# Projecting the second memory's keys and values beside the norms of the even and the odd layer

## The reference, cut to what matters

```python
mem_n = rmsnorm(mem, g_mem)                       # once, for both layers
# in the even and in the odd layer:
mk, mv = jnp.split(mem_n @ w_mem_kv, 2, axis=-1)  # 256 x 1024 @ 1024 x 1024
sc = einsum('bshd,bmhd->bhsm', q, mk) * HEAD_DIM ** -0.5
out = einsum('bhsm,bmhd->bshd', softmax(sc), mv)
```

## Time and profile before

| | |
|---|---|
| timed runs, us | 3944.46, 3948.77, 3956.41 |
| profiled execution, us | 3957.16 |
| its span, us | 3955.3 |
| TensorE clock, mean over the span | 0.945 of full |
| TensorE, VectorE, GpSimd, ScalarE busy, us | 3541.3, 1811.4, 1580.2, 897.8 |
| eight chunks of the first section, from the span's start | 306.9 to 879.0 |
| post norm and even norm | 2162 to 2246.9 |
| odd norm | 3298.7 to 3338.4 |

### The profile page before, as it was taken

One profiled execution on the slowest core, in us unless ns is written; L12 is line 12 of the kernel. 1 busy time (PEld: TensorE's weight loads), 2 busy tenths in 40 slices (PEclk: granted clock), 3 DMA queues, 4 the chain that ended last, 5 costly groups with the idle time before them and its releaser, 6 DMA issues.

```text
span 3955.3 us, 44173 instructions
## 1 busy us (share of the span) xinstructions
PE 3541.3 (90%) x16732; PEld 2842.2 (72%) x16732; DVE 1811.4 (46%) x2344; ACT 897.8 (23%) x1667; POOL 1580.2 (40%) x2013
## 2 busy tenths in 40 slices
PE   7998999999988999979899698779868988989988
PEld 6777998877766667767667387667656766778867
DVE  5763223227794454653531646464534343122343
ACT  3242112123012442323101222222221122120021
POOL 3543453224692224534454154243313433334423
PEclk9998899999999999989899899889878999999999
DMA  3121122112122012131121110000002101111211
GB/s 111 52 67 54 56 65 62 51 54 75 51 83 74 19 35 59 40 96 38 47 91 43 56 43 27 22 27 27 27 11 77 48 27 43 46 52 40 78 38 64
DMA packets 300662, 205.36 MB, mean 52 GB/s; under 512 B 25749, under 2 KB 277657, under 8 KB 300473
## 3 DMA queue, kind: packets, MB, share of 16 engines
q1 hardware_dynamic: 271241, 132.77, 12.2%
q10 hardware_dynamic: 29232, 69.95, 4.8%
HBM read 173.06 MB, written 29.63 MB: 51 GB/s over the span
## 4 chain that ended last, share of the span: by engine, by line
PE 71%; DVE 15%; ACT 5%; issue 3%; POOL 3%; ACTq 1%; DMA 1%; PEld 1%; DVEq 0%; PEldq 0%; POOLq 0%
PE ps L348 53%; PE ps L1308 5%; PE ps L784 3%; DVE wrk L650 3%; DVE wrk L629 2%; ACT wrk L812 2%; POOL w_lo L2453 2%; PE ps L797 1%; PE ps L1666 1%; PE ps L523 1%; POOL w_hi L2448 1%; PE ps L1985 1%; DVE wrk L837 1%; DVE small L840 1%; PE ps L676 1%
## 5 line engine op out<-in xcount | busy, mean ns | idle before, releaser
L2448 POOL TENSOR_TENSOR w_hi<-w_raw,pool_one 128x256 fp32r<-128x256 f32 x1004 | 687.4, 713 | 2322.6 <-PE ps L348 2305.6
L348 PE MATMUL ps<-h_hi,w_hi 128*128 128x512 f32 x2928 | 1210.0, 413 | 97.2 <-POOL w_lo L2453 23.7
L348 PE MATMUL ps<-h_lo,w_hi 128*128 128x512 f32 x2928 | 1157.8, 395 | 0.0
L348 PE MATMUL ps<-h_hi,w_lo 128*128 128x512 f32 x2928 | 1157.7, 395 | 0.0
L2453 POOL TENSOR_TENSOR w_lo<-w_raw,w_hi 128x256 fp32r<-128x256 f32 x1004 | 893.4, 918 | 23.2
L348 PEld LDWEIGHTS ps<-h_hi,w_hi 128*128 128x128 f32 x2928 | 560.4, 191 | 280.6 <-issue 105.7
L348 PEld LDWEIGHTS ps<-h_hi,w_lo 128*128 128x128 f32 x2928 | 559.5, 191 | 122.1
L348 PEld LDWEIGHTS ps<-h_lo,w_hi 128*128 128x128 f32 x2928 | 561.5, 192 | 112.8 <-issue 8.9
L348 PE MATMUL ps<-y_hi,w_hi 128*128 128x512 f32 (+1 forms) x896 | 349.6, 390 | 30.5 <-issue 29.7
L348 PE MATMUL ps<-y_hi,w_lo 128*128 128x512 f32 (+1 forms) x896 | 335.1, 374 | 0.0
L348 PE MATMUL ps<-y_lo,w_hi 128*128 128x512 f32 (+1 forms) x896 | 334.9, 374 | 0.0
(11 more groups left out here) (335 smaller groups left out, 3807.5 us busy)
## 6 DMA issues: line engine op xcount, KB each, us to landing
w_raw<-in_w_in SPq DMA_DIRECT2D x87, 512.0 KB
w_raw<-in_even_w_in SPq DMA_DIRECT2D x48, 512.0 KB
away<-wrk ACTq DMA_DIRECT2D x80, 256.0 KB, 2.0
wrk<-away ACTq DMA_DIRECT2D x32, 512.0 KB
w_raw<-in_odd_w_in SPq DMA_DIRECT2D x32, 512.0 KB
wrk<-in_x ACTq DMA_DIRECT2D x16, 512.0 KB, 8.2
w_raw<-in_w_br SPq DMA_DIRECT2D x32, 256.0 KB
w_raw<-in_even_w_out SPq DMA_DIRECT2D x24, 256.0 KB
```

The source lines that it names most:

```text
L348: mm = nc.tensor.matmul(ps[:, b, 0:n], l, r, start=(k == 0 and q == 0), stop=(k == nk - 1 and q == 2))
L2448: ins = nc.gpsimd.tensor_tensor(hi, raw, one[:, 0:2], ALU.mult)
```

## The change

The projection for E stays in the first section. That for the even layer moves to a new thread order in the section of the post norm: `dense` holds it (planned 76 us) and then `head v`; `aux` holds post norm and even norm (40 us each). That for the odd layer stands in `dense` of the odd norm's section (planned 46 us), with the norm in `aux`. The second memory's normalised rows stay in float32 in `wrk` 8 and 9, are stored to DRAM (1 MB) and fetched twice, each time rounded by ScalarE and split by VectorE. The reloaded x now goes into `y_hi` and `y_lo` after the E merge and is turned into `wrk` 0 to 7. `AHEAD_PACE` is 2.6.

```diff
-AHEAD_PACE = 2.0
+AHEAD_PACE = 2.6
...
-    def memory_kv(name, w_kv, which):
+    def memory_kv(name, w_kv, which, out, there, us):
...
-                pe.wait_ge(mem_normed.sem, mem_normed.nth(0))
+                pe.wait_ge(*there)
...
-            stage(name, AHEAD_PACE * dense_us(r, P), ("pe",), pe=f_pe, act=f_act)
+            stage(name, us / 2, ("pe",), pe=f_pe, act=f_act)
...
-    at_kv = [memory_kv("E k v", weights("w_mem_kv"), 0), memory_kv("even k v", weights("even_w_mem_kv_2"), 1),
-             memory_kv("odd k v", weights("odd_w_mem_kv_2"), 1)]
+    at_kv = [memory_kv("E k v", weights("w_mem_kv"), 0, wt(10), (mem_normed.sem, mem_normed.nth(0)),
+                       2 * AHEAD_PACE * 20.8)]
...
+            def emit(ch, k, b, root, src=src):
+                ch.link(nc.vector.scalar_tensor_tensor(src(k, b), src(k, b), col("g_mem_2", k), root, ALU.mult, ALU.mult))
+        norm("memory norm", src, P, emit, sq=6, rs=7, us=30.0, bank=6)
+    def m_store(act):
+        act.dma_start(mem_kept, wrk[:, 8:10, :]).then_inc(mem_stored, 16)
...
     def x_back(act):
-        tiles_gated(act)
+        out_ready(act, merge_e.t0 + merge_e.n - 1, 1)
         for n in range(NX):
-            act.dma_start(wt(n), x_tiles[n]).then_inc(x_again, 16)
+            act.dma_start(x_token_row(n), x_tiles[n]).then_inc(x_again, 16)
...
+    def mem_fetch(act, first, n):
+        act.dma_start(wrk[:, first:first + 2, :], mem_kept).then_inc(mem_back, 16)
+    def mem_round(act, first, n):
+        act.wait_ge(mem_back, 16 * (n + 1))
+        for j in range(2):
+            nc.scalar.activation(y_hi[:, 2 + j, :], wt(first + j), ACT.Copy).then_inc(mem_rounded.sem, 1)
+    def mem_part(dve, first, n):
+        for j in range(2):
+            dve.wait_ge(mem_rounded.sem, mem_rounded.nth(2 * n + j))
+            nc.vector.tensor_tensor(y_lo[:, 2 + j, :], wt(first + j), y_hi[:, 2 + j, :].bitcast(F32),
+                                    ALU.subtract).then_inc(mem_parted.sem, 1)
...
     section()
     on("dense")
+    at_kv.append(memory_kv("even k v", weights("even_w_mem_kv_2"), 1, y_spare[:, 0, :], mem_there(0), 76.0))
+    on("aux")
...
     norm("post norm", acc_at, HALF, post, sq=8, rs=9)
...
-    section()
-    on("dense")
     h_parted = norm_acc("even norm", "even_norm_g_2")
-    on("aux")
+    on("side")
...
-    rope(0, r_qk, 50.4)
+    rope(0, r_qk, 3.4)
...
+    def mem_load_again(act):
+        act.wait_ge(m_done.sem, m_done.nth(7))
+        mem_fetch(act, 7, 1)
+        yield 0.95
+        out_ready(act, r_om.t0 + r_om.n - 1, 1)
+        mem_round(act, 7, 1)
...
     section()
     on("dense")
+    at_kv.append(memory_kv("odd k v", weights("odd_w_mem_kv_2"), 1, wt(1), mem_there(1), 46.0))
+    on("aux")
...
     h_parted = norm_acc("odd norm", "odd_norm_g_2")
+    on("dense")
```

More of the change, by code:

```diff
@@ L1142, in f_act @@
                         out_ready(act, r.t0 + j, b)
[L1143 to L1144 removed]
+                        dst = out[:, j * MEM + b * P:j * MEM + (b + 1) * P] if kind == 0 else \
+                            out[:, b * HALF + j * P:b * HALF + (j + 1) * P]
                         nc.scalar.activation(dst, ps[:, b, 0:P], ACT.Copy).then_inc(dense_free[b], 1)
@@ L1239, in _hybrid @@
         src = lambda k, b: mem_t[:, k, b * P:(b + 1) * P]
[L1240 to L1243, removed]
+        if which == 0:
+            emit = split_emit(src, lambda k: col("g_mem", k), lambda k, b: mem_view(y_hi, 0)[:, k, b * P:(b + 1) * P],
+                              lambda k, b: mem_view(y_lo, 0)[:, k, b * P:(b + 1) * P], P, tmp=7, first=2 * P)
+        else:
+            def emit(ch, k, b, root, src=src):
[3 more added lines that the diff above has]
+        act.dma_start(mem_kept, wrk[:, 8:10, :]).then_inc(mem_stored, 16)
+    stage("second memory stored", 0.5, act=m_store)
     def memories_there(dve):
@@ L1835, in post @@
         ch.link(nc.vector.scalar_tensor_tensor(y, y, col("g_post", k), root, ALU.mult, ALU.mult))
-        ch.link(nc.vector.tensor_tensor(y, y, x_row(k)[:, b * HALF:(b + 1) * HALF], ALU.add))
+        ch.link(nc.vector.tensor_tensor(y, y, wt(k, b), ALU.add))
     norm("post norm", acc_at, HALF, post, sq=8, rs=9)
@@ L1858, in spill @@
         loads_done(act)
-    stage("x stored, rotary tables back", 30.0, act=spill)
+        for b in range(2):
+            room(act, b)
+    stage("post norm", 41.0)
+    stage("x stored, rotary tables back", 42.0, act=spill)
     w2 = weights("even_w_in_2")
@@ L2187, in _hybrid, with even_sum, mem_part_again, even_there @@
     m_done = gate_z("even memory z", run(2, *both(w2, C2_Z + 2 * W)), lambda j, b: wt(4 + j, b), None, 10)
-    add_out("even out M", run(4, *both(w2o[2], 0), 4, 4), gated_in(m_done))
+    r_om = run(4, *both(w2o[2], 0), 4, 4)
+    add_out("even out M", r_om, gated_in(m_done))
+    even_summed = sig.take("even_summed", 1)
+    def even_sum(dve):
+        dve.drain().then_inc(even_summed.sem, 1)
+    stage("even summed", 0.1, dve=even_sum)
+    on("aux")
[5 more added lines that the diff above has]
+        mem_round(act, 7, 1)
+    def mem_part_again(dve):
+        yield 0.95
+        mem_part(dve, 7, 1)
+    stage("even memory gated", 46.0)
+    stage("second memory in parts", 50.0, act=mem_load_again, dve=mem_part_again)
     section()
     on("dense")
+    at_kv.append(memory_kv("odd k v", weights("odd_w_mem_kv_2"), 1, wt(1), mem_there(1), 46.0))
+    on("aux")
+    def even_there(act):
+        act.wait_ge(even_summed.sem, even_summed.nth(0))
+    stage("even summed", 0.1, act=even_there)
     h_parted = norm_acc("odd norm", "odd_norm_g_2")
+    on("dense")
     w3 = weights("odd_w_in_2")
@@ L2196, in _hybrid, with kv_sent @@
     r_ov = run(4, *both(w3, C3_V))
-    project("odd v", r_ov, to_tiles(0), ready=part_ready(h_parted))
+    def kv_sent(act, j, b):
+        if j == 1:
+            room(act, b)
+    project("odd v", r_ov, to_tiles(0), ready=part_ready(h_parted), before=kv_sent)
     section()
```

37 lines of the change are left out of this document (27 added, 10 removed).

## The result

The kernel after takes 4003.36 us (median of 4 runs, 4002.43 to 4005.72), the kernel before beside it 3950.61 (3944.46 to 3956.41): a ratio of 1.0135, 95% interval 1.0123 to 1.0147. It is slower, 53 us by the medians, where the prediction's sum had 15, and it lies above the range of 3924 to 3998. The profiled span is 4001.5 us against 3955.3, that is 46.2 us more.

A forecast was written before the change was run, and what follows sets the result against it. TensorE was taken as the bound, except at chunk heads and in the norms' gaps. The terms -50 (first section), +25 (post and even norm) and +40 (odd norm) gave +15 us: 3964 us on the median's scale, range 3924 to 3998.

The forecast's parts named there:

- the first section: Eight chunks and the work ahead of them, relieved of two layers' projections: 50 us gained, bounds 27 and 83 us.
- post and even norm: Even layer's projection beside these two norms: 25 us lost through uncovered groups and slowed VectorE, bounds 15 and 40 us.
- the odd norm: Odd layer's projection beside this norm: 40 us lost, nearly all its TensorE time staying visible, bounds 28 and 46 us.
- I take 3 us per chunk for this: Chunk heads in the first section: TensorE stands about 4.1 us, the clock falls, and a chunk takes 65.5 us.
- my own formula: First section's chunk: 68.8 us less 8.8 of dense work, plus some 2.5 lost in gaps, gives 62.5 us.
- "5 us" ahead of the chunks: Between A's projection and the first reciprocal of A's norm: 2.0 tiles of dense work instead of 2.5, 5 us gained.
- The second half's groups are covered: Post and even norm: groups in the second half's squares hide behind VectorE's 15.4 us of work on the first half.
- the collision: In the norms GpSimd's splits slow VectorE by 2.8 us a tile: 11 us at post and even, about 5 at odd.
- 25 groups are left, 16.2 us: Odd norm: groups of products still to do after the last sum, 16.2 us, before `odd v` can start.
- the third rival: VectorE and GpSimd exclude each other fully in the norms and chunks stay near 68 us: +43, 3992 us; chance 0.15.
- 1 us back: Post and even norm: the moved groups keep TensorE warmer than before, gaining 1 us.
- The gain's rival: Chunks follow TensorE's work to 62 us without clock falls, norms take 22 and 38 us: -23, 3926 us; chance 0.22.

The follow-up runs named there:

- e1_yield: Kernel after, each of ScalarE's 16 roundings in the even and odd norm given its own due point so evictions can go between: 3970.39 us, ratio 1.0037.
- e1b_early: As e1_yield, with the first half's eight roundings also placed among ScalarE's squares of the second half: 3958.52 us, ratio 1.0012 to the kernel before.
- e5_tiny: Kernel after, with GpSimd splitting only one element of each tile of the second memory's projections: 3992.45 us, ratio 1.0087.
- e2: Kernel after, products planned over 26 us (odd) and 66 us (even) so every eviction stands ahead of the first rounding: 4003.39 us, ratio 1.0111.
- v2: As v1, with the moved products kept out of the time before the first root of post, even and odd norm: 3957.28 us, ratio 1.0009.
- v7: Kernel after with only the even layer's projection moved, roundings as in e1b_early, keys in 256-column products, pace 2.43: 3915.54 us, ratio 0.989.
- e10: As v2, with GpSimd splitting only one element of each tile of the second memory's projections: 3935.68 us, ratio 0.9948.
- v1: As e1b_early, with rounding and splitting of the normalised rows moved into even out M: 3952.13 us, ratio 0.999.

## Why the prediction was wrong

**The direction was right, and the size was not.** The first section gives less than TensorE's work removed, and the norms cover little of what they get. Against the sum the first section gave 22 us more (72 for 50), post and even norm cost 22 more (46.6 for 25), the odd norm 32 more (71.7 for 40): -72 + 46.6 + 71.7 = +46 us by the spans, where +15 stood. The two errors in the norms add up, and the one in the first section hides a part of them.

**The first section** was put at 50 us and gave 72. The term that failed is "I take 3 us per chunk for this" (the falls of the clock at the heads): the chunks take 62.2 us, and without that term my own formula gives 62.5. That these agree so closely is luck in part. The 68.8 us that it starts from is the longer of two clean chunks, whose mean is 67.1; from there, less 8.8, it would be 58.3, and the two clean chunks now take 60.0 in the mean. The other six, at 0.92 to 0.97 of the clock, take 61.3 to 65.9. TensorE's waits at the heads are 27.7 us in all, 3.5 a chunk, near the 4.1 of the prediction. Chunks under 63 us were one of its own signs of being wrong. "5 us" ahead of the chunks came out as 5 (first reciprocal of A's norm at 234.3 instead of 239.4).

**Post and even norm** were put at 25 us and cost 46.6. The step that failed: "The second half's groups are covered: VectorE needs 3.35 + 8 x 1.5 = 15.4 us for the first half meanwhile." In the post norm, which has no rounding, VectorE does work meanwhile, and this norm's 12.6 us are near its terms, 7.7 us of groups and a share of the collision. In the even norm it cannot get beyond its third tile before the last root. The row that shows it was in the trace of before (VectorE idle 3.7 us until L581, in either norm); I read the durations of the two halves and not what stands between them on ScalarE. Behind that the same 16 roundings hold the last evictions, and the first tile of `head v` starts after the norm. e1_yield and e1b_early show both parts.

**The odd norm** was put at 40 us and cost 71.7. "25 groups are left, 16.2 us" was right in number (the trace has 120 products, 20 groups, behind the norm) and wrong in place and price: they run after VectorE's part, not beside it, and at half clock, 25.9 us. So the step that failed is the same: ScalarE's 16 roundings, and not TensorE's work, set when the last groups can run. The other terms held: a half of the squares took 21.5 us (20.2 predicted), the wait for the stores 2.9 (3), the four more splits 3.4 of VectorE's time ("about 5 us more"), the later start 3.5 ("some 2.5 us more than now"). The terms given add up to 46 us for the last sum and not to 49 (2.5 + 3 + 2 x 20.2); and the lower bound of the first section comes out as 28 to 30 us and not as 27. Neither decides anything.

**The collision** was put at 11 and 5 us and measured as 13.0 in the traces, 11 to 19 by e5_tiny; the third rival's full exclusion is refuted: beside GpSimd VectorE's L1880 takes 911 ns instead of 692, while the splits run on. In the 37 us of that view (2106.8 to 2143.8) its 32 instructions on tiles and the 24 of the splits would need 39 us one after the other at their lengths of the earlier trace rows, and GpSimd still had 8.4 us idle. The Trainium skill (SBUF — State Buffer, "Who interferes with whom") has an exclusive lock here; by these rows it is a slowdown.

**The clock** stood in my sum as "1 us back". The 120 products behind the odd norm took 25.9 us at half clock; at 0.112 us each they would take 13.4, so the clock cost some 12 us there alone. e2 and v2 show stretches of 48 and 40 us with narrow products at half speed. I had the rows for this (20 products in 4 us at 0.50) and used them only for the first section.

The gain's rival named a chunk of 63.5 us as the point from which it decides. The chunks went below it, and the kernel became slower all the same, since all of it hung on norms of 22 and 38 us. The cause of the missed norms is shown by the placing of the roundings, with its control, for 37 to 41 us; what of the rest the pace of 2.6 makes is not known.

## What to carry to other kernels

Work planned beside a chain overlaps only if every engine that touches it may switch between the two: look for instructions issued in one piece (here 16 roundings on ScalarE), and ask for each eviction or root what stands ahead of it there. Price narrow products at both clocks, and ask whether the tiles for them arrive in time where the engine that prepares them is slowed. A changed amount of work in a planned thread must be judged with its pace set anew: the wide keys were worth nothing at 2.0 and, with the pace, 28 us at 2.2, and v7 lost 23 us when 2.43 became 2.6. Run the pace on the kernel without the edit too.

## What the runs showed of the hardware

Products of 128 columns alone can stay at half clock for long, though TensorE is busy without a gap: 25.9 us in the kernel after (window at 0.50), 40 us in v2. The same products held full clock for 27 us in e10. Neither is a rule: behind the stand of 4.1 us the kernel after came back to full clock among such products after some 3 us, e2 with longer runs of them after 48.

A wait of 0.57 us in v2 and one of 0.53 in v1 stood ahead of a fall; one of 0.53 in e1b_early did not bring one. So no length of a wait that lowers the clock is shown; e10 removes the waits together with GpSimd's load.

From start to start a product of 128 columns takes 0.112 us at full clock (v2, 3284 to 3288) and 0.213 at half (v2, 3322 to 3329). VectorE and GpSimd slow each other when both work on tiles in SBUF: 692 to 911 ns and 752 to 906 ns on VectorE, 612 to 960 and 724 to 1040 ns on GpSimd.
